# Gathering and adding the first twelve expert picks between the last query-weight tiles of a one-core Trainium2 kernel

## Chip, cores and metric

The kernel runs on one core of a Trainium2 chip. The metric is the device time of one execution in microseconds. The engines are called PE (matrix), DVE (vector), ACT (scalar), POOL (GpSimd) and SP (which only issues transfers). Each runs its own program in order and meets the others at semaphores. A difference under 0.2% of the time, some 7 us, can't be told from no change.

## The reference

Two transformer-like blocks run over 512 tokens of width 1024. The change lies in the expert layer of the first one, between the mixing output and the final norm of that block:

```python
def chunk(t):                                   # 128 tokens
    qh = (t @ w_q).reshape(T, 8, 2, 128)        # 1024 -> 2048 query features
    s = einsum('thpd,hpnd->thpn', qh, sub_keys) # 128 keys for each of 8 heads x 2 halves
    s_top, i_top = top_k(s, 16)
    cand = s_top[:, :, 0, :, None] + s_top[:, :, 1, None, :]
    best, pos = top_k(cand.reshape(T, 8, 256), 16)
    idx = ...                                   # 8 x 16 = 128 experts for each token
    g = softmax(best)
    ue, ve = u_tab[idx], v_tab[idx]             # 16384 experts x 1024, twice
    act = gelu(einsum('thkd,td->thk', ue, t))
    return einsum('thk,thkd->td', g * act, ve)
```

## The kernel before, in words

**The ring of weights.** All linear layers draw weight tiles of 1024x128 from one stream. SP loads tile n into slot n % 4 of `w32` as soon as POOL has split tile n-4. POOL splits each tile into a high and a low part (`split_tile`, L391 to L401, two instructions), once PE has finished tile n-4 (`tile_done`). PE multiplies a tile with `linear` (L474): 24 products of 128x128 by 128x512, which wait for the split of their own tile (`w_split`) and read the activations `xhi` and `xlo`.

**The query section, "pq".** It has 16 tiles m = 0 to 15. PE does the first four as one group. From then on it runs `linear` of tile m, then `key_scores(m - 1)` (L676), and for m = 4 to 7 also the turning of the tokens into rows. ACT copies each product (L1029), then the scores of the tile before (L1125). DVE finds the best keys of the first 128 tokens (`top_keys`, `top_pairs`, `pick_experts`, L1645 to L1698) as soon as four tiles of scores are there, which gives the indices of picks 0 to 31.

**The picks.** There are 512 picks: 4 groups of 128 tokens by 128 experts. For pick p POOL issues one indirect transfer (`gather`, L428), in which each of 128 partitions fetches its expert's row of `u` and of `v`, 8 KB together (1,048,576 bytes a pick). DVE makes the dot of `u` with the token (`expert_dot`, L1719). ACT makes gelu (L1158), the weight (L1162) and a diagonal matrix (L1167) of it (`expert_weight`). PE multiplies the diagonal with `v` into two banks that sum over 128 picks (`expert_sum`, L712, four recorded products a pick) and signals `pick_used`. There are eight slots for the fetched rows. They overlay split activations: `slots[0]` to `slots[3]` lie on `yhi` and `ylo`, which nobody reads any more once the section "mix" is running; `slots[4]` to `slots[7]` lie on `xhi` and `xlo`, which the query products read until tile 15 is done. A gather into a used slot waits for the `pick_used` of the pick before it there.

**The order at the seam.** POOL splits all query tiles up to number 15, then issues gathers 0 to 3, then waits at gather 4 until PE has done all 16 query tiles. ACT makes the softmax of the first 32 picks (`gates_exp(0)`, L1151) only after its last query copy; DVE waits for it before its first dot. PE does pick 0 after `key_scores(15)`. Four more weight tiles are split within the gather loop at picks 16, 24, 32 and 40, sixteen more from pick 298 on. After the last pick follow the norm and the second block. They need the sum of all picks.

Of the kernel before, what the change touches and what calls it, by code (L numbers as in the profile page):

```python
# [6 lines left out]
ALU = mybir.AluOpType  # L7
# [6 lines left out]
P = 128  # L14
# [18 lines left out]
NPICKS = T // P * PICKS  # L33
UNITS = NPICKS // UNIT
MEM_AT, MEM_EVERY = 288, 8
FF = 4096
WINDOWS = (2, 4, 8, 16)
MIX_ORDER = (1, 0, 3, 2, 5, 4, 7, 6)
# [71 lines left out]


SECTIONS, DONE, NTILES = plan()


SEMAPHORES = (
# [20 lines left out]
def build(nc, a, out):  # L136
    ctx = ExitStack()
    with ctx:
# [5 lines left out]
        def sem(name):  # L144
            return sems[name]
# [77 lines left out]
        look = flat_acc[:, 1536:2048]  # L223
        tokens = work[:, :, :].rearrange("p k t -> p (k t)").rearrange("p (t d) -> p t d", t=TT)
        dot_out = ar(12288, 1024)
        diag = flat_acc[:, 512:768].rearrange("p (a n) -> p a n", a=2)

        def peer_tokens(t):
            return tiles_of(8192 if t < 2 else 4096, 2, T)
# [36 lines left out]
        def bank(b):  # L266
            return psum[:, b, :]
# [118 lines left out]
        @block.gpsimd  # L386
        def _(pool):
            pool.memset(zeros[:, :], 0.0).then_inc(sem("zeros_set"), 1)
            pool.wait_ge(sem("zeros_set"), 1)

            def split_tile(s, n, nth, reused):  # L391

                pool.wait_ge(w_loaded[s], nth * 16)
                if reused:
                    pool.wait_ge(tile_done, n + 1 - RING)
                hi = whi[:, s, :, :].rearrange("p k n -> p (k n)")
                lo = wlo[:, s, :, :].rearrange("p k n -> p (k n)")
                pool.tensor_tensor(hi, w32[:, s, :], zeros[:, :].broadcast_to((P, 1024)), ALU.add)\  # L398
                    .then_inc(sem("w_upper"), 1)
                pool.wait_ge(sem("w_upper"), n + 1)  # L400
                pool.tensor_tensor(lo, w32[:, s, :], hi.bitcast(F32), ALU.subtract).then_inc(w_split, 1)  # L401

            for s in range(RING):
                split_tile(s, s, 1, False)

            def split_tiles(first, end):

                up, down = -(-first // RING), end // RING
                for n in range(first, up * RING):
                    split_tile(n % RING, n, n // RING + 1, True)  # L410
                with pool.Fori(up, down) as g:
                    for s in range(RING):
                        split_tile(s, g * RING + s, g + 1, True)
                for n in range(down * RING, end):
                    split_tile(n % RING, n, n // RING + 1, True)

            mixed = first_tile("pool") + RING
            n = first_tile("memk")
            split_tiles(RING, n)

            def gather(p):
                if p % UNIT == 0:
                    pool.wait_ge(sem("picked"), p // UNIT + 1)
                if p >= SLOTS:
                    pool.wait_ge(sem("pick_used"), p - SLOTS + 1)
                elif p == 4:
                    pool.wait_ge(tile_done, n)
                pool.indirect_dma_start(  # L428
                    out=slots[p % SLOTS], out_offset=None, in_=a["experts"],
                    in_offset=bass.IndirectOffsetOnAxis(ap=indices[:, p:p + 1], axis=0),  # L430
                ).then_inc(sem(f"experts_in{p % SLOTS}"), 16)

            for p in range(NPICKS):
                gather(p)
                if 16 <= p < 48 and p % 8 == 0:
                    m = (p - 16) // 8
                    split_tile((n + m) % RING, n + m, (n + m) // RING + 1, True)
                m = (p - MEM_AT - 10) // MEM_EVERY
                if p >= MEM_AT + 10 and (p - MEM_AT - 10) % MEM_EVERY == 0 and m < 2 * KB:
                    split_tile((n + RING + m) % RING, n + RING + m, (n + RING + m) // RING + 1, True)  # L440
            split_tiles(n + RING + 2 * KB, mixed)

            step = Steps(pool, "pool_step")
            pool.wait_ge(sem("affine_done"), 8 * 6 + 1)
            step(pool.memset(ppad_odd[:, :, 0:16], 0.0))
            step.settle()
            for i in range(0, 6, 2):
                k = MIX_ORDER[i]
                pool.wait_ge(sem("affine_done"), 8 * 6 + i + 1)
                mix_window(pool, step, k, ppad_odd, pool_y_odd, False)  # L450
                step(pool.tensor_tensor(yhi[:, k, :], pool_y_odd, zeros[:, :].broadcast_to((P, T)), ALU.add))
                step.settle()
                pool.tensor_tensor(ylo[:, k, :], pool_y_odd, yhi[:, k, :].bitcast(F32), ALU.subtract)\  # L453
                    .then_inc(sem("odd_split"), 1)
                pool.wait_ge(sem("odd_split"), i // 2 + 1)
            split_tiles(mixed, NTILES)
# [3 lines left out]
        def _(pe):  # L460
# [219 lines left out]
            def turn_tokens(t):  # L680
# [3 lines left out]
                for half in range(2):  # L684
# [6 lines left out]
                        mm = pe.matmul(dst, xlo[:, 4 * half + k, t * P:(t + 1) * P], identr, start=False, stop=True)  # L691
                    mm.then_inc(sem("tokens_turned"), 1)

            linear_group(n, range(o, o + 4), (sem("split2"), 0))
            for m in range(3):
                key_scores(m)
            for m in range(4, HP):
                linear(n + m, o + m)
                key_scores(m - 1)
                if m < 8:  # L700
                    turn_tokens(m - 4)
            key_scores(HP - 1)

            def expert_sum(p):

                t, c = p // PICKS, p % PICKS
                if c == 0:
                    pe.wait_ge(sem("peer_copied"), 2 * t) if t else pe.wait_ge(sem("tokens_copied"), 2 * TT)
                pe.wait_ge(sem("diagonal"), p + 1)
                v = slots[p % SLOTS][:, D:2 * D]  # L710
                for half in range(2):
                    mm = pe.matmul(bank(4 + half), diag[:, p % 2, :], v[:, half * T:(half + 1) * T], start=(c == 0),  # L712
                                   stop=(c == PICKS - 1))
                mm.then_inc(sem("pick_used"), 1)

            def turn_peer(t):

# [31 lines left out]

            MH, ML = (lambda k: mem_hi[:, k, :]), (lambda k: mem_lo[:, k, :])  # L750
            n, o = SECTIONS["memk"]
            for p in range(NPICKS):
                expert_sum(p)
                if p % PICKS == PICKS - 1:
                    turn_peer(p // PICKS)
                m, at = (p - MEM_AT) // MEM_EVERY, (p - MEM_AT) % MEM_EVERY
                if 0 <= m < 2 * KB and at == 0:
                    linear(n + m, o + m, MH, ML, CT, ready=(sem("mem_split"), 0) if m == 0 else None)
                if KB <= m < 2 * KB and at == 4:
                    pe.wait_ge(sem("peer_added"), 8 * (p // PICKS))  # L760
                    turn_copied(m - KB, SECTIONS["memv"][1], mem_raw, CT // P, 2)
# [217 lines left out]
        def _(act):  # L979
# [47 lines left out]
            def copy_product(dst, o, cols=T, func=ACT.Copy, **more):  # L1027
                wait_product(act, o)
                free(act.activation(dst, bank(o % RING)[:, 0:cols], func, **more), o)  # L1029
# [102 lines left out]
                    act.activation(tokens[:, t, half * T:(half + 1) * T], bank(4 + half), ACT.Copy)\  # L1132
                        .then_inc(sem("tokens_copied"), 1)

            act.wait_ge(sem("split2"), 8)
            for m in range(HP):
                if m >= 2:
                    act.wait_ge(sem("key_scores"), m - 1)
                copy_product(acc[:, m % 2, :], o + m)
                if m:  # L1140
                    scores_copy(m - 1)
                if 5 <= m < 9:
                    tokens_copy(m - 5)
            scores_copy(HP - 1)
            act.wait_ge(sem("key_scores"), HP)
            act.dma_start(memT, a["memT"].rearrange("(k p) t -> p k t", p=P)).then_inc(sem("mem_in"), 16)

            def gates_exp(u):
                act.wait_ge(sem("best_ready"), u + 1)
                for h in range(2):  # L1150
# [4 lines left out]
            def expert_weight(p):  # L1155
# [8 lines left out]
                act.wait_ge(sem("weighed"), p + 1)  # L1164
                if p >= 2:
                    act.wait_ge(sem("pick_used"), p - 1)
                act.activation(diag[:, p % 2, :], ident, ACT.Copy, scale=weights[:, c:c + 1])\  # L1167
                    .then_inc(sem("diagonal"), 1)

            def peer_copy(t):  # L1170
                act.wait_ge(sem("pick_used"), PICKS * (t + 1))
# [10 lines left out]
                    .then_inc(sem("values_copied"), 1)  # L1182

            n, o = SECTIONS["memk"]
            gates_exp(0)
            for p in range(NPICKS):
                expert_weight(p)
                if p % PICKS == PICKS - 1:
                    peer_copy(p // PICKS)
# [172 lines left out]
        def _(dve):  # L1362
# [346 lines left out]

            def expert_dot(p):  # L1710
                c = p % (2 * UNIT)
                dve.wait_ge(sem(f"experts_in{p % SLOTS}"), 16 * (p // SLOTS + 1))
                if p == 0:
                    dve.wait_ge(sem("tokens_copied"), 2 * TT)
                else:
                    dve.wait_ge(sem("dotted"), p)
                if p >= 2 * UNIT:
                    dve.wait_ge(sem("gelu_ready"), p - 2 * UNIT + 1)
                dve.scalar_tensor_tensor(dot_out, slots[p % SLOTS][:, 0:D], 1.0, tokens[:, p // PICKS, :], ALU.mult,  # L1719
                                         ALU.mult, accum_out=inner[:, c:c + 1]).then_inc(sem("dotted"), 1)  # L1720

            def add_peer(t):
# [422 lines left out]
```

## Time and profile before

| what | value |
|---|---|
| median of 3 runs | 3493.74 us (3491.2 to 3499.36) |
| the profiled execution, its time | 3496.58 us |
| its span | 3494.8 us |
| granted clock of PE, mean over the span | 0.928 |
| PE / DVE / POOL / ACT busy | 84% / 65% / 53% / 26% |
| ACT copies the products of query tiles 12 and 15 | at 642.36 and 661.84 us |
| pick phase, first gather after tile 15 to last gather | 662.0 to 1980.5 us |

The span is counted from the first instruction of the profile to the last; the time of the same execution is 1.8 us more. The profiled execution lies 2.8 us above the median of the runs. All stages named here by times are in us from the span's start. The granted clock is 1.0 for 2.4 GHz and 0.5 for 1.2 GHz; a busy product is not a product at its peak, since products overlap in the record.

### The profile page before, as it was taken

Reading aid. Unit: us, or ns where it says so; the run is one execution under the profiler, and the core shown is the slowest. Engines: PE = TensorE matmul, PEld = TensorE weight load, DVE = VectorE, ACT = ScalarE, POOL = GpSimd, SP = SyncE. Lnnn points to the kernel's source line nnn. Section 1 sums busy time; section 2 is a strip of 40 time slices with the busy share of each in tenths; the row PEclk is TensorE's granted clock in tenths of the full one; section 3 lists DMA queues with packets and bytes.
Section 4 is the critical chain, followed back from the end, with each engine's and each line's share of the span. In section 5 each row is a group of like instructions: output and inputs, shape, how many; then the busy total and the mean of one; then the engine's idle time right before and its main releaser. Section 6 shows DMA issues by size and latency. Waiting matters only on the chain. (4 is left out here: it accounts for less than half of the span.)

```text
span 3494.8 us, 33128 instructions
## 1 busy us (share of the span) xinstructions
PE 2945.1 (84%) x10628; PEld 1938.5 (55%) x10628; DVE 2257.4 (65%) x3761; ACT 926.1 (26%) x2350; POOL 1856.1 (53%) x1099
## 2 busy tenths in 40 slices
PE   6889898877778877888877779979899975889998
PEld 5667676632333323444433267657678864667886
DVE  7793464376666667776766583675855577586556
ACT  2115402233433333333333322221200012220001
POOL 2544375464444444666554264254577763557874
PEclk9899899999999999999999989989999987999998
DMA  5531122699999999999999811011122220112221
GB/s 216 185 113 55 43 79 73 241 421 419 413 418 412 412 422 409 391 389 399 390 422 418 341 66 55 31 60 61 60 90 96 91 72 12 61 60 93 94 96 55
DMA packets 126107, 719.21 MB, mean 206 GB/s; under 512 B 13200, under 2 KB 16400, under 8 KB 60176
## 3 DMA queue, kind: packets, MB, share of 16 engines
q0 software_dynamic: 73728, 536.90, 37.4%
q1 hardware_dynamic: 46560, 161.18, 13.4%
q10 hardware_dynamic: 5680, 19.40, 1.5%
q8 instruction: 72, 1.18, 0.1%
q14 instruction: 67, 0.55, 0.0%
HBM read 715.33 MB, written 2.10 MB: 205 GB/s over the span
## 5 line engine op out<-in xcount | busy, mean ns | idle before, releaser
L712 PE MATMUL psum<-slots,acc 128*128 128x512 f32 x2048 | 1016.2, 643 | 267.9 <-ACT acc L1167 267.4
L398 POOL TENSOR_TENSOR whi<-w,zeros 128x1024 fp32r<-128x1024 f32 x277 | 548.1, 1979 | 883.1 <-PE psum L469 566.4
L428 POOL DMA_INDIRECT slots<-in_experts,consts x512 | 564.1, 1102 | 675.0 <-PE psum L712 603.5
L1719 DVE SCALAR_TENSOR_TENSOR arena<-slots,work 128x1024 f32<-128x1024 f32 x512 | 663.2, 1295 | 400.1 <-DMA slots<-in_experts,consts 383.1
L712 PEld LDWEIGHTS psum<-slots,acc 128*128 128x128 f32 x2048 | 393.7, 202 | 868.5 <-ACT acc L1167 462.3
L401 POOL TENSOR_TENSOR wlo<-w,whi 128x1024 fp32r<-128x1024 f32 x277 | 718.2, 2593 | 21.7
L467 PE MATMUL psum<-xhi,whi 128*128 128x512 f32 x1104 | 451.5, 409 | 8.7 <-POOL wlo L401 5.6
L468 PE MATMUL psum<-xlo,whi 128*128 128x512 f32 x1104 | 441.8, 400 | 0.0
L469 PE MATMUL psum<-xhi,wlo 128*128 128x512 f32 x1104 | 440.5, 399 | 0.0
L467 PE MATMUL psum<-yhi,whi 128*128 128x512 f32 (+1 forms) x736 | 300.1, 408 | 49.9 <-POOL ylo L453 20.7
L468 PE MATMUL psum<-ylo,whi 128*128 128x512 f32 (+1 forms) x736 | 296.2, 402 | 0.0
L469 PE MATMUL psum<-yhi,wlo 128*128 128x512 f32 (+1 forms) x736 | 296.1, 402 | 0.0
L1158 ACT ACTIVATE consts<-consts 128x1 f32<-128x1 f32 x512 | 101.7, 199 | 585.2 <-DVE arena L1719 578.2
L1167 ACT ACTIVATE acc<-consts 128x128 f32<-128x128 f32 x512 | 205.5, 401 | 185.8 <-PE psum L712 172.0
L467 PEld LDWEIGHTS psum<-xhi,whi 128*128 128x128 f32 x1104 | 211.0, 191 | 66.5 <-issue 16.0
L469 PEld LDWEIGHTS psum<-xhi,wlo 128*128 128x128 f32 x1104 | 210.5, 191 | 52.0
L468 PEld LDWEIGHTS psum<-xlo,whi 128*128 128x128 f32 x1104 | 210.9, 191 | 50.5 <-issue 1.7
L1347 ACT ACTIVATE work<-psum,vecs 128x512 f32<-128x512 f32 x64 | 44.1, 689 | 579.9 <-PE psum L469 419.3
L467 PEld LDWEIGHTS psum<-yhi,whi 128*128 128x128 f32 x736 | 142.4, 193 | 92.3 <-issue 32.1
L1984 DVE TENSOR_TENSOR work<-work 128x512 f32<-128x512 f32 x64 | 108.5, 1695 | 113.8 <-ACT work L1347 113.8
L1998 DVE TENSOR_TENSOR acc<-acc,psum 128x512 f32<-128x512 f32 x112 | 75.4, 685 | 161.1 <-PE psum L469 160.9
L469 PEld LDWEIGHTS psum<-yhi,wlo 128*128 128x128 f32 x736 | 143.1, 194 | 34.6
(266 smaller groups left out, 3671.3 us busy)
## 6 DMA issues: line engine op xcount, KB each, us to landing
w<-in_stream SPq DMA_DIRECT2D x277, 512.0 KB
arena<-in_wmod SPq DMA_DIRECT2D x4, 2048.0 KB, 17.8
arena<-in_wmod ACTq DMA_DIRECT2D x8, 1024.0 KB, 6.1
acc<-in_wmod ACTq DMA_DIRECT2D x8, 1024.0 KB, 8.3
slots<-in_experts,consts POOLq DMA_INDIRECT x512
xres<-in_xT SPq DMA_DIRECT2D x1, 2048.0 KB, 15.3
outT<-xres SPq DMA_DIRECT2D x8, 256.0 KB, 2.0
consts<-in_consts SPq DMA_DIRECT2D x1, 1056.0 KB, 5.2
```

Source lines behind the costliest of these rows:

```text
L398: pool.tensor_tensor(hi, w32[:, s, :], zeros[:, :].broadcast_to((P, 1024)), ALU.add)\
L401: pool.tensor_tensor(lo, w32[:, s, :], hi.bitcast(F32), ALU.subtract).then_inc(w_split, 1)
L428: pool.indirect_dma_start(out=slots[p % SLOTS], out_offset=None, in_=a["experts"], in_offset=bass.IndirectOffsetOnAxis(ap=indices[:, p:p + ...
L467: pe.matmul(dst, hi, xh(k), start=(j == 0), stop=False)
L468: pe.matmul(dst, hi, xl(k), start=False, stop=False)
L469: mm = pe.matmul(dst, lo, xh(k), start=False, stop=(j == len(ks) - 1))
L712: mm = pe.matmul(bank(4 + half), diag[:, p % 2, :], v[:, half * T:(half + 1) * T], start=(c == 0), stop=(c == PICKS - 1))
L1158: act.activation(gelus[:, c:c + 1], inner[:, c:c + 1], ACT.Gelu).then_inc(sem("gelu_ready"), 1)
L1167: act.activation(diag[:, p % 2, :], ident, ACT.Copy, scale=weights[:, c:c + 1])\
L1719: dve.scalar_tensor_tensor(dot_out, slots[p % SLOTS][:, 0:D], 1.0, tokens[:, p // PICKS, :], ALU.mult, ALU.mult, accum_out=inner[:, c:c + ...
L1984: step(dve.tensor_tensor(q, t, t, ALU.mult))
L1998: free(dve.tensor_tensor(acc[:, k, :], acc[:, k, :], bank(oo % RING), ALU.add), oo)
```

## The change

The first twelve picks use only `slots[0]` to `slots[3]`, three times each; from pick 12 on the slots go round as before. POOL splits the query tiles only up to number 11 ahead. Then it issues gathers 0 to 3, splits tile 12, issues gathers 4 and 5, splits tile 13, issues 6 and 7, splits tile 14, issues 8 and 9, splits tile 15, issues 10 and 11, and goes on from pick 12. Gather 4 waits until pick 0 has been added, gather 5 for pick 1, and so on. PE adds picks 0 and 1 after the product of tile 12 and `key_scores(11)`, picks 2 and 3 after tile 13, 4 and 5 after tile 14, 6 and 7 after tile 15, and the rest as before. ACT makes the softmax of the first 32 picks at tile 9, and the weights of two picks after each of tiles 12 to 15. The diagonals of the first twelve picks have a place of their own, since the old one is the buffer of the query copies. DVE's order stays as it is.

```diff
--- before.py
+++ after.py
@@ -33,6 +33,7 @@
 NPICKS = T // P * PICKS
 UNITS = NPICKS // UNIT
 MEM_AT, MEM_EVERY = 288, 8
+FIRST, FIRST_AT = 12, 12
 FF = 4096
 WINDOWS = (2, 4, 8, 16)
 MIX_ORDER = (1, 0, 3, 2, 5, 4, 7, 6)
@@ -112,6 +113,20 @@
 SECTIONS, DONE, NTILES = plan()
 
 
+def slot_uses():
+
+    slots = [p % 4 if p < FIRST else (p - FIRST + 4) % SLOTS for p in range(NPICKS)]
+    before, uses, last = [], [], {}
+    for p, slot in enumerate(slots):
+        before.append(last.get(slot))
+        uses.append(slots[:p + 1].count(slot))
+        last[slot] = p
+    return slots, before, uses
+
+
+SLOT, SLOT_BEFORE, SLOT_USES = slot_uses()
+
+
 SEMAPHORES = (
     "tile_done", "early_done", "bank_free0", "bank_free1", "bank_free2", "bank_free3", "w_loaded0", "w_loaded1",
     "w_loaded2", "w_loaded3", "w_split", "consts_in", "vecs_in", "ctx_in", "conds_in", "mod_dot", "mod_in0",
@@ -223,7 +238,10 @@
         look = flat_acc[:, 1536:2048]
         tokens = work[:, :, :].rearrange("p k t -> p (k t)").rearrange("p (t d) -> p t d", t=TT)
         dot_out = ar(12288, 1024)
-        diag = flat_acc[:, 512:768].rearrange("p (a n) -> p a n", a=2)
+        diags = [t.rearrange("p (a n) -> p a n", a=2) for t in (ar(9216, 256), flat_acc[:, 512:768])]
+
+        def diag(p):
+            return diags[p >= FIRST][:, p % 2, :]
 
         def peer_tokens(t):
             return tiles_of(8192 if t < 2 else 4096, 2, T)
@@ -416,21 +434,28 @@
 
             mixed = first_tile("pool") + RING
             n = first_tile("memk")
-            split_tiles(RING, n)
 
             def gather(p):
                 if p % UNIT == 0:
                     pool.wait_ge(sem("picked"), p // UNIT + 1)
-                if p >= SLOTS:
-                    pool.wait_ge(sem("pick_used"), p - SLOTS + 1)
-                elif p == 4:
-                    pool.wait_ge(tile_done, n)
+                if SLOT_BEFORE[p] is not None:
+                    pool.wait_ge(sem("pick_used"), SLOT_BEFORE[p] + 1)
+                else:
+                    pool.wait_ge(tile_done, n if p >= FIRST else first_tile("mix"))
                 pool.indirect_dma_start(
-                    out=slots[p % SLOTS], out_offset=None, in_=a["experts"],
+                    out=slots[SLOT[p]], out_offset=None, in_=a["experts"],
                     in_offset=bass.IndirectOffsetOnAxis(ap=indices[:, p:p + 1], axis=0),
-                ).then_inc(sem(f"experts_in{p % SLOTS}"), 16)
-
-            for p in range(NPICKS):
+                ).then_inc(sem(f"experts_in{SLOT[p]}"), 16)
+
+            early = first_tile("pq") + FIRST_AT
+            split_tiles(RING, early)
+            for p in range(4):
+                gather(p)
+            for m in range(4):
+                split_tile((early + m) % RING, early + m, (early + m) // RING + 1, True)
+                for p in range(4 + 2 * m, 6 + 2 * m):
+                    gather(p)
+            for p in range(FIRST, NPICKS):
                 gather(p)
                 if 16 <= p < 48 and p % 8 == 0:
                     m = (p - 16) // 8
@@ -691,6 +716,18 @@
                         mm = pe.matmul(dst, xlo[:, 4 * half + k, t * P:(t + 1) * P], identr, start=False, stop=True)
                     mm.then_inc(sem("tokens_turned"), 1)
 
+            def expert_sum(p):
+
+                t, c = p // PICKS, p % PICKS
+                if c == 0:
+                    pe.wait_ge(sem("peer_copied"), 2 * t) if t else pe.wait_ge(sem("tokens_copied"), 2 * TT)
+                pe.wait_ge(sem("diagonal"), p + 1)
+                v = slots[SLOT[p]][:, D:2 * D]
+                for half in range(2):
+                    mm = pe.matmul(bank(4 + half), diag(p), v[:, half * T:(half + 1) * T], start=(c == 0),
+                                   stop=(c == PICKS - 1))
+                mm.then_inc(sem("pick_used"), 1)
+
             linear_group(n, range(o, o + 4), (sem("split2"), 0))
             for m in range(3):
                 key_scores(m)
@@ -699,19 +736,10 @@
                 key_scores(m - 1)
                 if m < 8:
                     turn_tokens(m - 4)
+                if m >= FIRST_AT:
+                    expert_sum(2 * (m - FIRST_AT))
+                    expert_sum(2 * (m - FIRST_AT) + 1)
             key_scores(HP - 1)
-
...
 
             def turn_peer(t):
 
@@ -749,7 +777,7 @@
 
             MH, ML = (lambda k: mem_hi[:, k, :]), (lambda k: mem_lo[:, k, :])
             n, o = SECTIONS["memk"]
-            for p in range(NPICKS):
+            for p in range(2 * (HP - FIRST_AT), NPICKS):
                 expert_sum(p)
                 if p % PICKS == PICKS - 1:
                     turn_peer(p // PICKS)
@@ -1132,19 +1160,6 @@
                     act.activation(tokens[:, t, half * T:(half + 1) * T], bank(4 + half), ACT.Copy)\
                         .then_inc(sem("tokens_copied"), 1)
 
...
-
             def gates_exp(u):
                 act.wait_ge(sem("best_ready"), u + 1)
                 for h in range(2):
@@ -1164,8 +1179,26 @@
                 act.wait_ge(sem("weighed"), p + 1)
                 if p >= 2:
                     act.wait_ge(sem("pick_used"), p - 1)
-                act.activation(diag[:, p % 2, :], ident, ACT.Copy, scale=weights[:, c:c + 1])\
+                act.activation(diag(p), ident, ACT.Copy, scale=weights[:, c:c + 1])\
                     .then_inc(sem("diagonal"), 1)
+
+            act.wait_ge(sem("split2"), 8)
+            for m in range(HP):
+                if m >= 2:
+                    act.wait_ge(sem("key_scores"), m - 1)
+                copy_product(acc[:, m % 2, :], o + m)
+                if m:
+                    scores_copy(m - 1)
+                if 5 <= m < 9:
+                    tokens_copy(m - 5)
+                if m == 9:
+                    gates_exp(0)
+                if m >= FIRST_AT:
+                    expert_weight(2 * (m - FIRST_AT))
+                    expert_weight(2 * (m - FIRST_AT) + 1)
+            scores_copy(HP - 1)
+            act.wait_ge(sem("key_scores"), HP)
+            act.dma_start(memT, a["memT"].rearrange("(k p) t -> p k t", p=P)).then_inc(sem("mem_in"), 16)
 
             def peer_copy(t):
                 act.wait_ge(sem("pick_used"), PICKS * (t + 1))
@@ -1182,8 +1215,7 @@
                     .then_inc(sem("values_copied"), 1)
 
             n, o = SECTIONS["memk"]
-            gates_exp(0)
-            for p in range(NPICKS):
+            for p in range(2 * (HP - FIRST_AT), NPICKS):
                 expert_weight(p)
                 if p % PICKS == PICKS - 1:
                     peer_copy(p // PICKS)
@@ -1709,14 +1741,14 @@
 
             def expert_dot(p):
                 c = p % (2 * UNIT)
-                dve.wait_ge(sem(f"experts_in{p % SLOTS}"), 16 * (p // SLOTS + 1))
+                dve.wait_ge(sem(f"experts_in{SLOT[p]}"), 16 * SLOT_USES[p])
                 if p == 0:
                     dve.wait_ge(sem("tokens_copied"), 2 * TT)
                 else:
                     dve.wait_ge(sem("dotted"), p)
                 if p >= 2 * UNIT:
                     dve.wait_ge(sem("gelu_ready"), p - 2 * UNIT + 1)
-                dve.scalar_tensor_tensor(dot_out, slots[p % SLOTS][:, 0:D], 1.0, tokens[:, p // PICKS, :], ALU.mult,
+                dve.scalar_tensor_tensor(dot_out, slots[SLOT[p]][:, 0:D], 1.0, tokens[:, p // PICKS, :], ALU.mult,
                                          ALU.mult, accum_out=inner[:, c:c + 1]).then_inc(sem("dotted"), 1)
 
             def add_peer(t):
```

## Rows read from the trace of the kernel before

**Rows 1.** The page: DMA busy tenths, the span in 40 equal slices.

```profile
DMA  5531122699999999999999811011122220112221
```

**Rows 2.** Stretches: length, busy of each engine, granted clock, DMA share, GB/s.

```profile
611.00:616.00 5.00, 5.00 (x23) 4.04 (x22) 0.00 (x0) 0.00 (x0) 0.00 (x0) 1.00 0.32 105
655.00:662.00 7.00, 7.00 (x38) 5.86 (x37) 0.00 (x0) 1.36 (x3) 0.00 (x0) 1.00 0.01 5
...
663.00:1983.00 1320.00, 1052.30 (x2453) 443.69 (x2453) 910.91 (x2029) 503.33 (x1646) 659.29 (x547) 0.93 1.00 410
1950.00:1980.00 30.00, 23.95 (x49) 8.13 (x48) 14.79 (x24) 10.95 (x37) 11.26 (x12) 1.00 1.01 421
```

**Rows 3.** Waits, 600 to 2000 us: total, times, longest.

```profile
DVE small L1702 <- ACT consts L1151: 63.9, 1, 63.9
```

**Rows 4.** POOL's timeline: start, length, [idle before, releaser].

```profile
608.62 2.37 POOL L401 TENSOR_TENSOR wlo<-w,whi 128x1024 fp32r<-128x1024 f32 x1
616.37 1.89 POOL L398 TENSOR_TENSOR whi<-w,zeros 128x1024 fp32r<-128x1024 f32 x1 [5.38 <-PE psum L469]
...
622.93 1.89 POOL L398 TENSOR_TENSOR whi<-w,zeros 128x1024 fp32r<-128x1024 f32 x1 [2.18 <-PE psum L469]
624.90 2.40 POOL L401 TENSOR_TENSOR wlo<-w,whi 128x1024 fp32r<-128x1024 f32 x1
```

**Rows 5.** POOL's timeline at the seam and after it.

```profile
640.46 1.17 POOL L428 DMA_INDIRECT slots<-in_experts,consts  x1 [0.17 <-issue]
...
644.42 0.93 POOL L428 DMA_INDIRECT slots<-in_experts,consts  x1 [0.30 <-issue]
662.01 0.94 POOL L428 DMA_INDIRECT slots<-in_experts,consts  x1 [16.66 <-PE psum L469]
...
687.91 1.16 POOL L428 DMA_INDIRECT slots<-in_experts,consts  x1 [0.77 <-PE psum L712]
689.63 0.94 POOL L428 DMA_INDIRECT slots<-in_experts,consts  x1 [0.56 <-PE psum L712]
```

**Rows 6.** DVE's timeline: the first indices, and what follows them.

```profile
603.13 0.18 DVE L1698 CAST consts<-consts 128x32 uint32<-128x32 f32 x1
667.21 0.17 DVE L1702 RECIPROCAL small<-small 128x2 f32<-128x2 f32 x1 [63.90 <-ACT consts L1151]
```

**Rows 7.** ACT's timeline: copies of tile 12 and 13, and the first weight.

```profile
642.36 0.60 ACT L1029 ACTIVATE acc<-psum 128x512 f32<-128x512 f32 x1 [5.06 <-PE psum L469]
643.19 0.60 ACT L1125 ACTIVATE arena<-psum 128x512 f32<-128x512 f32 x1 [0.23 <-PE psum L676]
648.85 0.60 ACT L1029 ACTIVATE acc<-psum 128x512 f32<-128x512 f32 x1 [5.06 <-PE psum L469]
...
667.19 1.28 ACT L1158 ACT_TABLE_LOAD   x1
668.90 0.20 ACT L1158 ACTIVATE consts<-consts 128x1 f32<-128x1 f32 x1 [0.42 <-DVE arena L1719]
```

**Rows 8.** PE's timeline: after key scores 15, and after a short pause.

```profile
670.07 11.24 PE L712 MATMUL psum<-slots,acc 128*128 128x512 f32 x20 [5.53 <-ACT acc L1167]
...
697.12 11.38 PE L712 MATMUL psum<-slots,acc 128*128 128x512 f32 x20 [4.57 <-ACT acc L1167]
```

**Rows 9.** Stretches again, columns as in rows 2: products at either clock.

```profile
544.00:548.00 4.00, 4.00 (x10) 3.12 (x10) 3.90 (x9) 2.15 (x3) 0.00 (x0) 0.50 0.00 0
550.00:554.00 4.00, 4.00 (x19) 3.22 (x18) 3.90 (x9) 1.64 (x2) 0.00 (x0) 1.00 0.18 25
...
668.00:675.00 7.00, 4.93 (x6) 2.18 (x7) 6.58 (x14) 3.56 (x12) 0.67 (x1) 0.51 1.02 416
675.00:680.00 5.00, 5.00 (x13) 2.23 (x12) 4.79 (x31) 1.19 (x4) 2.14 (x3) 1.00 1.03 374
```

**Rows 10.** POOL's timeline: the last two gathers.

```profile
1977.99 0.94 POOL L428 DMA_INDIRECT slots<-in_experts,consts  x1 [1.54 <-PE psum L712]
1980.47 0.94 POOL L428 DMA_INDIRECT slots<-in_experts,consts  x1 [1.55 <-PE psum L712]
```

More of the change, by code:

```diff
@@ L701, in _ @@
                     turn_tokens(m - 4)
+                if m >= FIRST_AT:
+                    expert_sum(2 * (m - FIRST_AT))
+                    expert_sum(2 * (m - FIRST_AT) + 1)
             key_scores(HP - 1)
[L704 to L714, printed above, removed]
             def turn_peer(t):
@@ L1133, in tokens_copy @@
                         .then_inc(sem("tokens_copied"), 1)
[L1135 to L1146, printed above, removed]
             def gates_exp(u):
```

## The prediction

> **What bounds the kernel now.** I read the page's slices first, since one busy share can't speak for a program of so many stages. The DMA digits stand at 9 for fourteen slices, from the ninth to the 22nd, and at 2 or less nearly everywhere after that [rows 1]. That block is the pick phase. The table by stretches then says how full it is: over the 1320 us from 663 to 1983 the DMA engines are busy with share 1.00 at 410 GB/s, and with share 1.01 at 421 GB/s near the end, while no engine is full [rows 2]. A gather is 1,048,576 bytes, so at 421 GB/s it should take 2.49 us; the last two are issued 2.48 us apart [rows 10]. So from the first gather after tile 15 (662.01) to the last (1980.47) the chip moves bytes and the rest follows. What sets the time of this phase is when it starts and how many gathers are left by then.
>
> Before it, the query section is bound by PE: ACT's copies of tiles 12 and 13 come 6.49 us apart, each after 5.06 us of idleness that PE ends [rows 7]. POOL's splits have slack here: it waits 5.38 and 2.18 us for PE before it may split [rows 4]. The DMA is idle at the end of it (share 0.01 from 655 to 662) [rows 2], because four gathers were issued by 645.35 and the fifth, at 662.01, waits for tile 15 [rows 5]. The indices for all of them had been there since 603.31; DVE then sat 63.90 us until ACT came to the softmax [rows 3, 6]. So there is room: some 50 us in which twelve gathers (30 us of transfer) would fit. The question is what the new order makes of PE's section.
>
> **The change part by part.** *Gathers 0 to 3 earlier.* POOL is done with tile 11 at 608.62 + 2.37 = 610.99 and idle until 616.37, when tile 8 is done [rows 4]. Four issues took 640.46 to 645.35, 4.89 us [rows 5]. They fit into that gap of 5.38 us, so split 12 stays at 616.37 and costs nothing; the DMA has share 0.32 there [rows 2]. They are four gathers that before too had landed before 655, so they save nothing by themselves.
>
> *Softmax at tile 9.* Two small exponentials and a table load, in ACT's idle of about 5 us a tile [rows 7]. Zero; if it were not hidden, 2 us. DVE's dots 0 to 3 then run long before PE wants them; gather 4 will be issued at 648 and its dot is wanted at about 684, so DVE, which has its next top-k work behind that dot, is covered too. The gelu table load of 1.28 us [rows 7] moves between the score copy and the first weight, where PE waits for it: once 1.28 us.
>
> *The new waits on POOL.* This is the part that decides. Gather 4 waits for pick 0, gather 5 for pick 1, and both come after PE's product of tile 12. Behind them in POOL's order stands the split of tile 13, which before ran at 622.93, twenty microseconds ahead of PE [rows 4, 7]. PE's next product waits for that split. So after each pair of picks PE, POOL and ACT run one after the other. From ACT's copy of one tile to the copy of the next:
>
> - copy to end of the score copy: 643.19 + 0.60 - 642.36 = 1.43 us [rows 7]
> - gelu, weight, diagonal, first product of PE: 670.07 - 668.90 = 1.17 us [rows 7, 8]
> - two picks on PE: twice 689.63 - 687.91 = 1.72, so 3.44 us (gathers that wait for slots follow PE's picks at that distance) [rows 5]
> - issue of the odd gather: 0.95 us [rows 5]
> - split: 624.90 + 2.40 - 622.93 = 4.37 us [rows 4], and 0.1 us to PE (my estimate)
> - the 24 products to the copy: 6.49 less the 0.83 between copy and score copy = 5.66 us [rows 7]
>
> That is 17.1 us in place of 6.49.
>
> *The clock.* In each round PE is idle for 0.95 + 4.37 + 0.1 = 5.4 us before its products. When PE had been idle for 5.53 us, the granted clock was 0.51 over 668 to 675, though PE worked again from 670.07, and 1.00 in the stretch after [rows 8, 9]. The same products come 10 in 4 us at clock 0.50 and 19 in 4 us at 1.00 [rows 9]. PE so loses half of some 4.9 us, 2.4 us a round. With it a round is 19.5 us. (The Trainium skill, "TensorE: Matmul & The Clock Gate", section "Seeing it yourself", warns that clock records have been unreliable. If they were so here, the term would vanish and the sum be that of the first rival below; the count of products agrees with the records.)
>
> *The sum up to the saturated phase.* Copy 12 stays at 642.36. Copy 13 comes after 19.5 + 1.28 at 663.1, copy 14 at 682.6, copy 15 at 702.1 (before 661.84). Pick 6 is added 1.43 + 1.17 + 1.72 later, at 706.5, and there gather 10 is issued. Gather 11 follows 1.7 us later, and 12 to 15 at once behind it, since tile 15 is done. Gathers 16 and 17 need picks 8 and 9, which landed long ago and are added by about 715; six gathers are 15 us of transfer, so the DMA doesn't run dry. Had this cover gone, each gather that came late would cost its 2.5 us. From gather 10 on the phase is as full as it was from gather 4 at 662.01.
>
> *What is given back.* Six gathers (4 to 9) are already done by then: 6 x 2.48 = 14.9 us [rows 10]. (By the Trainium skill, "DMA: Bandwidth & Descriptors", section "Anatomy of one DMA", bytes move at 436 GB/s: 2.40 us a gather, an estimate by which 14.4 us would come back and the sum be half a microsecond more.) The bounds of this term: 0, if they save nothing, and 6 x 1320/508 = 15.6 us, the average over the 508 gathers, which holds other transfers as well [rows 2, 5].
>
> Start of the phase 706.5 - 662.0 = +44.5, less 14.9: **+29.6 us**. Everything behind the phase shifts with it unchanged. Of the +44.5, 31.9 us are three rounds that grew by 10.6, 7.2 us the clock, 1.3 us the table, and the rest is that the saturated phase now starts behind the sum of pick 6 and not at tile 15 itself. Against the profiled execution, 3496.58 + 29.6 = 3526.2 us; that execution lies 2.8 us above the median of the runs, so **3523.3 us**, which I round to 3523.
>
> **The rivals.**
>
> - *No clock fall.* Before the pauses seen, PE had other work behind it than it will have now, so it might keep its clock over 5.4 us. Then +22.4 us, 3516. Against it: a pause of 4.57 us within the picks was followed by five picks in 11.38 us, as slow as the first five (11.24), where the pace of 1.72 gives 8.6 [rows 8].
> - *A deeper fall.* PE also idles 3.1 us between key scores 11 and pick 0, and the clock may not recover before the next pause. The bound is a tile wholly at half clock, 5.66 instead of 2.4 lost, thrice 3.3, and 2.7 us for slow first picks [rows 8]: +42 us at most, 3536; halfway 3530.
> - *The early gathers save nothing.* If the phase's length hung on something other than bytes, the delay would come through whole: +44.5, 3538. Against it stands share 1.00 over 1320 us [rows 2].
> - *Not slower: a fuller stream.* The mean rate of the phase is 410 GB/s and its best 421 [rows 2]. If the picks done ahead left DVE, ACT and PE so far in front that no burst of top-k work or split ever thins the stream again, the phase would take 1320 x 410/421, 34.5 us less: -5 us, 3489. It decides from 419.5 GB/s on, where the gain is 29.6. Against it: from pick 12 on the slots and their waits are the same as before, so the lead over the DMA is again eight slots at most, and the share is already 1.00.
>
> That the change doesn't do what it says is not open: POOL's waits stand in program order ahead of the splits.
>
> **How the numbers follow.** Chances: forecast 0.68, no clock fall 0.14, deeper fall 0.10, nothing saved 0.05, fuller stream 0.03. The range starts at 3512, below the no-fall case by 4 us for a split, an issue or a latency that is shorter than its row, and ends at 3533, between the forecast and the deep end of the second rival; outside are half of that rival and the last two, some 0.14. One per cent is 35 us, and 0.2% is 7 us, which is about what can be told from no change: only the fuller stream, and a delay that I overlooked a cover for, lie there. Slower 0.95, same 0.03, faster 0.02.
>
> **What the profile after would show.** Right: gathers 0 to 3 at 611 to 616; the splits of tiles 13, 14 and 15 at about 650.6, 670 and 689, each right behind a gather, with PE's products waiting for them (a wait of PE on the low split, three times, about 5 us each); PE's clock near 0.5 in the first 5 us of each of these tiles; gather 10 at about 706 and the last gather at about 2010; GB/s in the phase still 410. Wrong: splits that run ahead of the picks; a phase whose rate differs by more than 1%; or products at full clock after the pauses.

## Result and profile after

The changed kernel takes 3524.79 us (median of 6 runs, 3517.37 to 3530.16) against 3492.47 us for the kernel before (6 runs): a ratio of 1.0092, 95% interval 1.0076 to 1.0108, or +32.3 us where +29.6 was worked out. Timed a second time, beside other runs of the kernel before, it took 3527.41 us against 3490.84 us, ratio 1.01 (1.0084 to 1.0115), or +36.6 us. The profiled execution has a span of 3522.9 us. Its slices answer to [rows 1]; the block of nines begins as before in the ninth slice of a longer span:

```profile
DMA  5531122299999999999999911111122220112221
```

Single executions differ in what they need up to the seam: the copy of tile 12 lies at 642.36 us before the change and at 636.67 in this trace, and between 636 and 644 in those of the experiments that add no more than two picks before it. So I count from that copy.

POOL's timeline after, which answers to [rows 4] and [rows 5] (start, length, idle time before and what ended it):

```profile
605.54 1.17 POOL L445 DMA_INDIRECT slots<-in_experts,consts  x1 [0.17 <-issue]
...
610.75 1.89 POOL L416 TENSOR_TENSOR whi<-w,zeros 128x1024 fp32r<-128x1024 f32 x1 [0.32 <-PE psum L494]
612.72 2.41 POOL L419 TENSOR_TENSOR wlo<-w,whi 128x1024 fp32r<-128x1024 f32 x1
643.32 0.96 POOL L445 DMA_INDIRECT slots<-in_experts,consts  x1 [28.20 <-PE psum L727]
646.22 0.94 POOL L445 DMA_INDIRECT slots<-in_experts,consts  x1 [1.94 <-PE psum L727]
647.18 1.90 POOL L416 TENSOR_TENSOR whi<-w,zeros 128x1024 fp32r<-128x1024 f32 x1
649.15 3.22 POOL L419 TENSOR_TENSOR wlo<-w,whi 128x1024 fp32r<-128x1024 f32 x1
664.38 0.96 POOL L445 DMA_INDIRECT slots<-in_experts,consts  x1 [12.01 <-PE psum L727]
...
684.21 0.96 POOL L445 DMA_INDIRECT slots<-in_experts,consts  x1 [12.55 <-PE psum L727]
...
704.17 0.96 POOL L445 DMA_INDIRECT slots<-in_experts,consts  x1 [12.98 <-PE psum L727]
...
2004.94 0.94 POOL L445 DMA_INDIRECT slots<-in_experts,consts  x1 [1.54 <-PE psum L727]
```

Gathers 0 to 3 lie between the splits of tiles 11 and 12, where POOL stood idle before. Then POOL stands for 28.20 us at gather 4, with the split of tile 13 behind it. It stands for 12.01 us at gather 6 and for 12.55 us at gather 8, with the splits of tiles 14 and 15 behind them. The split of tile 13 starts 0.02 us after the issue of gather 5. Of the first twelve picks ten are gathered before gather 10, the first of the full phase, and six are added before tile 15 is done. ACT's copies of tiles 12 to 15 answer to [rows 7]:

```profile
636.67 0.60 ACT L1057 ACTIVATE acc<-psum 128x512 f32<-128x512 f32 x1 [5.06 <-PE psum L494]
659.78 0.60 ACT L1057 ACTIVATE acc<-psum 128x512 f32<-128x512 f32 x1 [18.50 <-PE psum L494]
679.62 0.60 ACT L1057 ACTIVATE acc<-psum 128x512 f32<-128x512 f32 x1 [16.70 <-PE psum L494]
699.58 0.60 ACT L1057 ACTIVATE acc<-psum 128x512 f32<-128x512 f32 x1 [16.83 <-PE psum L494]
```

Rounds of 23.11, 19.84 and 19.96 us stand where 6.49 was. PE's timeline shows the two pauses of a round, one before the picks and one before the next tile's products:

```profile
640.58 5.37 PE L727 MATMUL psum<-slots,arena 128*128 128x512 f32 x8 [3.11 <-ACT arena L1182]
652.42 0.80 PE L492 MATMUL psum<-xhi,whi 128*128 128x512 f32 x1 [6.48 <-POOL wlo L419]
...
662.12 3.70 PE L727 MATMUL psum<-slots,arena 128*128 128x512 f32 x8 [1.54 <-ACT arena L1182]
```

The waits of 600 to 712 us (total, times, longest) show how the second pause adds up, and DVE's wait for the softmax, which answers to [rows 3]:

```profile
DVE small L1734 <- ACT consts L1166: 23.0, 1, 23.0
...
PE psum L492 <- POOL wlo L419: 18.0, 3, 6.5
```

And the stretches (length, busy of PE, PEld, DVE, ACT, POOL with counts, granted clock, DMA share, GB/s), which answer to [rows 2] and [rows 9]:

```profile
643.00:646.00 3.00, 2.94 (x5) 0.86 (x3) 0.00 (x0) 0.00 (x0) 0.96 (x1) 0.62 0.36 66
...
672.00:676.00 4.00, 4.00 (x10) 3.13 (x11) 1.98 (x4) 0.00 (x0) 0.00 (x0) 0.50 0.40 135
676.00:680.00 4.00, 4.00 (x21) 3.32 (x21) 0.00 (x0) 0.38 (x1) 0.00 (x0) 1.00 0.02 4
...
710.00:2026.00 1316.00, 1041.91 (x2445) 437.87 (x2443) 904.14 (x1988) 497.31 (x1628) 648.82 (x538) 0.94 0.99 408
```

The products of tile 14 come 10 in 4 us at half clock, then 21 in 4 us; the first pair of picks is slowed too (0.62). The phase is as full as before: 408 against 410 GB/s.

The bill: from the copy of tile 12, gather 10 comes after 67.50 us, where gather 4 came after 19.65. That is +47.9. From there to the last gather it takes 1300.8 us in place of 1318.5, -17.7. In all +30.2 us. The rest of the two traces differs too: the copy of tile 12 comes 5.7 us earlier after the change, and behind the last gather the program takes 1518.0 us in place of 1514.3. These three terms add up to the 28.1 us between the spans. The last of them can't be charged to the change: over all traces of this case that rest takes 1514.3 to 1520.6 us, and the trace before is the shortest of them.

### The profile page after: what moved, and what is told of

Read it like the earlier page. It is cut to its first block and busy times, and to the rows that moved or that the text cites. A ratio compares the mean times of both kernels' runs of the same rounds, so it can differ in the third digit from the quotient of the medians.

```text
span 3522.9 us, 33122 instructions
## 1 busy us (share of the span) xinstructions
PE 2947.2 (84%) x10628; PEld 1941.8 (55%) x10628; DVE 2261.2 (64%) x3761; ACT 925.8 (26%) x2350; POOL 1855.0 (53%) x1099
## 5 line engine op out<-in xcount | busy, mean ns | idle before, releaser
L727 PE MATMUL psum<-slots,acc 128*128 128x512 f32 x2000 | 984.5, 639 | 264.3 <-ACT acc L1182 261.9
L1751 DVE SCALAR_TENSOR_TENSOR arena<-slots,work 128x1024 f32<-128x1024 f32 x512 | 673.2, 1315 | 464.7 <-DMA slots<-in_experts,consts 449.3
L727 PEld LDWEIGHTS psum<-slots,acc 128*128 128x128 f32 x2000 | 380.6, 200 | 847.3 <-ACT acc L1182 460.2
L493 PEld LDWEIGHTS psum<-ylo,whi 128*128 128x128 f32 x736 | 143.3, 195 | 33.9 <-issue 0.2
## 6 DMA issues: line engine op xcount, KB each, us to landing
arena<-in_wmod SPq DMA_DIRECT2D x4, 2048.0 KB, 17.7
```

The costliest lines, as they stand in the source:

```text
L493: pe.matmul(dst, hi, xl(k), start=False, stop=False)
L727: mm = pe.matmul(bank(4 + half), diag(p), v[:, half * T:(half + 1) * T], start=(c == 0), stop=(c == PICKS - 1))
L1751: dve.scalar_tensor_tensor(dot_out, slots[SLOT[p]][:, 0:D], 1.0, tokens[:, p // PICKS, :], ALU.mult, ALU.mult, accum_out=inner[:, c:c + 1] ...
```

## Experiments

Each was timed in several rounds beside runs of the kernel before on the same chip. Ratios are to that kernel, with 95% intervals.

**Splits ahead of the waiting gathers.** One edit to the changed kernel:

```diff
             for m in range(4):
                 split_tile((early + m) % RING, early + m, (early + m) // RING + 1, True)
-                for p in range(4 + 2 * m, 6 + 2 * m):
-                    gather(p)
+            for p in range(4, FIRST):
+                gather(p)
```

> The changed kernel with one edit: POOL splits the query tiles 12 to 15 before it waits at gather 4, and issues gathers 4 to 11 after them. Theory (the splits queued behind the waiting gathers make the rounds long): a round from ACT's copy of one tile to the next falls from 19.5 to 11.8 us (1.43 score copy, 1.17 to PE, 3.44 for two picks, 5.66 for the products), no clock fall before the products, gather 10 about 21 us later than the kernel before issued gather 4 (measured from the copy of tile 12), less 14.9 given back: +6 to +9 us against the kernel before, 25 us less than the changed kernel, near 3500 us. Rival (the rounds are long because of the picks themselves, on ACT and PE): within 3 us of the changed kernel, near 3525 us.

Measured: 3501.72 us against 3495.08, ratio 1.0017 (1.0008 to 1.0026), +6.6 us. ACT's copies in its trace:

```profile
642.59 0.60 ACT L1057 ACTIVATE acc<-psum 128x512 f32<-128x512 f32 x1 [5.06 <-PE psum L494]
...
657.56 0.60 ACT L1057 ACTIVATE acc<-psum 128x512 f32<-128x512 f32 x1 [10.35 <-PE psum L494]
...
669.29 0.60 ACT L1057 ACTIVATE acc<-psum 128x512 f32<-128x512 f32 x1 [8.60 <-PE psum L494]
...
681.01 0.60 ACT L1057 ACTIVATE acc<-psum 128x512 f32<-128x512 f32 x1 [8.59 <-PE psum L494]
```

The rounds are 14.97, 11.73 and 11.72 us long, with 11.8 expected. The first is 3.2 us longer than the others, which I hadn't allowed for: PE waits 3.11 us for the first diagonal in place of 1.54, and the first two picks take it 5.37 us in place of 3.70. Counted from the copy of tile 12, tile 15 is copied 24.5 us sooner than in the changed kernel, and the time against the kernel before falls from +32.3 to +6.6, within the +6 to +9 that I gave. The order of splits and gathers on POOL, with the clock falls that follow from it, makes some 25 us.

**Idle products in the pauses.** Behind each of the first three pairs:

```diff
                     expert_sum(2 * (m - FIRST_AT) + 1)
+                    if m + 1 < HP:
+                        for j in range(20):
+                            pe.matmul(bank(7), identr, xhi[:, j % KB, :], start=True, stop=True)
```

> The changed kernel with twenty products of no use (the identity by slices of xhi, into bank 7, which nobody reads then) behind each of the first three pairs of picks, 4.7 us at full clock, so that PE isn't idle while POOL splits. It adds work and changes no result. Theory (PE loses some 2 us a round to the lower clock after each pause): granted clock 1.0 in the products of tiles 13 to 15, 5 to 7 us less than the changed kernel, near 3519 us. Rival (the clock costs nothing that counts, or the fillers are in the way): the same as the changed kernel or up to 5 us more.

Measured: 3523.64 us against 3495.08, ratio 1.008 (1.0067 to 1.0094), where I had expected some 3519 us. The interval overlaps that of the changed kernel, so the time decides nothing. The trace says more. The same stretch of tile 14 as above, in this kernel:

```profile
672.00:676.00 4.00, 4.00 (x19) 3.22 (x18) 1.23 (x2) 0.00 (x0) 0.00 (x0) 1.00 0.28 110
```

The clock is full, and the rounds are 20.89, 17.90 and 17.65 us long, 6.5 less in all. So both kernels were timed again, beside each other:

> The changed kernel itself, so that the next run and it share a chip and the runs of the kernel before. +29 to +33 us against the kernel before, near 3524 us.

> The kernel with the idle products once more, beside the changed kernel. In the trace of its first run the rounds were 6.5 us shorter in all. Theory (the lower clock costs time on the path): 4 to 8 us less than the changed kernel in the same job. Rival (the shortened rounds are given back): within 2 us of it.

Measured: changed kernel 3527.41 us, ratio 1.01 (1.0084 to 1.0115), +36.6 us, above the +29 to +33 that I gave; with idle products 3519.26 us, ratio 1.0082 (1.0069 to 1.0095). The medians are 8.2 us apart and the rounds of the two traces 7.0 us (64.36 against 57.40 from the copy of tile 12 to that of 15). Both times the traces with idle products show the clock at 1.0 in the products of tiles 13 to 15, and rounds that are shorter by nearly the same amount. From the copy of tile 12 to the last gather these traces are 8.8 and 9.1 us shorter than those of the changed kernel. So useless work in the pauses shortens this stage, since PE then meets its real work at full clock. That the whole time falls with it is likely and no more, for the intervals of the ratios just overlap.

**No gather ahead.** One edit to the kernel before:

```diff
-                elif p == 4:
+                elif p == 0:
                     pool.wait_ge(tile_done, n)
```

> The kernel before with one edit: gathers 0 to 3 too wait until PE is done with query tile 15, so no pick is fetched ahead. Theory (the phase is bound by bytes and a gather done ahead of it is worth 2.48 us): four gathers more in the phase, +9.9 us against the kernel before, near 3502 us. Rival (what is fetched ahead saves nothing, the phase hangs on something else): 0 to +3 us.

Measured: 3504.16 us against 3495.08, ratio 1.0025 (1.0016 to 1.0034), +9.1 us by the medians. Four gathers moved into the full phase cost 2.3 us each. The credit for gathers done ahead is real.

**The front alone.** The changed kernel with `FIRST` = 4, all splits ahead, and sums and weights behind tile 15 as before:

```diff
-FIRST, FIRST_AT = 12, 12
+FIRST, FIRST_AT = 4, 12
...
-                if m >= FIRST_AT:
-                    expert_sum(2 * (m - FIRST_AT))
-                    expert_sum(2 * (m - FIRST_AT) + 1)
```

> The changed kernel with only its front: gathers 0 to 3 are issued ahead of split 12 and the softmax stands at tile 9, all splits run ahead, no pick is added and no fifth gather issued before tile 15 is done. Theory (these parts lie in idle time and save nothing, since the four gathers were through in time before too): -2 to +2 us against the kernel before, near 3494 us. Rival (the earlier dots of DVE and the softmax off the seam shorten the start of the phase): -5 us or more.

Measured: 3496.27 us against 3490.84, ratio 1.0009 (0.9999 to 1.0018). The medians are 5.4 us apart, outside the +-2 us I gave, but the interval holds 1. In its trace the way from the copy of tile 12 to the last gather is 3.0 us shorter than before (1335.1 for 1338.1), so time and trace point opposite ways. No gain from the earlier gathers and softmax can be seen in the time, and no loss that can be told from none.

**Weights a tile ahead, five pairs.** The splits as in the first experiment, sums at tiles 11 to 15 (`FIRST_AT` = 11), and on ACT:

```diff
-                if m >= FIRST_AT:
-                    expert_weight(2 * (m - FIRST_AT))
-                    expert_weight(2 * (m - FIRST_AT) + 1)
+                if FIRST_AT - 1 <= m < HP - 1:
+                    expert_weight(2 * (m + 1 - FIRST_AT))
+                    expert_weight(2 * (m + 1 - FIRST_AT) + 1)
```

> The changed kernel with the splits of tiles 12 to 15 ahead, and with ACT making the weights of a pair one tile before PE adds it: ACT at tiles 11 to 14 after the score copy, PE at tiles 11 to 15, five pairs in place of four. PE then should wait for nobody. Theory: tile 15 is done 4 x 3.44 = 13.8 us later than in the kernel before, gathers 4 to 11 (8 x 2.48 = 19.8 us) are through by then: -6 us against the kernel before, near 3486 us. Rival (a pick before tile 15 costs PE as much as it saves the DMA, since the phase has slack): 0 to +5 us.

> The kernel with five pairs and ready weights once more, beside the former on one chip and one set of runs of the kernel before: -6 to -10 us.

The edit puts ACT's weights at tiles 10 to 14; the first expectation names 11 to 14 for five pairs, which is a slip.

Measured: 3485.35 us against 3495.08, ratio 0.9975 (0.9963 to 0.9986), and again 3487.81 against 3494.16, ratio 0.9979 (0.9971 to 0.9988). It beats the kernel before by 6 to 10 us. In its first trace the tiles from 11 to 15 follow each other every 9.9 us on average, as 6.49 + 3.44 says, and PE's clock stays at 1.0 from 600 to 680 us. A part of that:

```profile
660.00:672.00 12.00, 12.00 (x54) 8.61 (x53) 4.79 (x10) 3.92 (x10) 2.90 (x3) 1.00 0.62 231
```

**Seven pairs.** The same with sums at tiles 9 to 15, sixteen picks in the four slots:

> As the kernel with ready weights, with seven pairs in place of five: softmax at tile 7, weights at tiles 8 to 14, sums at tiles 9 to 15, the first sixteen picks in the four free slots, splits always ahead of the gather that would block them. DVE's first dot waits for the first two token copies alone, its others follow it. Theory: tile 15 is done 6 x 3.44 = 20.6 us later than in the kernel before, twelve more gathers (29.8 us) are through: -9 us against the kernel before, near 3485 us, and some 3 us less than with five pairs. Rival (more picks ahead collide with the token turning or with DVE's first top-k work): no better than five pairs, or worse.

Measured: 3482.55 us against 3490.84, ratio 0.9975 (0.9967 to 0.9984): -8.3 us, where five pairs gave -9.7 and -6.4. Its trace showed a hole in the issues just when the last slots came free:

```profile
682.52 1.29 POOL L445 DMA_INDIRECT slots<-in_experts,consts  x1 [4.38 <-PE psum L498]
683.83 1.90 POOL L416 TENSOR_TENSOR whi<-w,zeros 128x1024 fp32r<-128x1024 f32 x1
685.81 3.22 POOL L419 TENSOR_TENSOR wlo<-w,whi 128x1024 fp32r<-128x1024 f32 x1
689.18 0.96 POOL L445 DMA_INDIRECT slots<-in_experts,consts  x1
```

> The kernel with seven pairs, and the four weight tiles that POOL splits among the gathers moved from picks 16, 24, 32, 40 to 24, 32, 40, 48. In the trace with seven pairs POOL issued one gather after tile 15 (682.5) and then split for some 5 us before the next (689.2), while the DMA ran dry. Theory (that hole ate what two more pairs brought): 3 to 6 us less than seven pairs, -11 to -14 us against the kernel before. Rival (the hole is made good within the phase): -8 us, as with five or seven pairs.

That the DMA ran dry in the hole was too strongly put: its share was 0.72, 0.79 and 0.74 in the three stretches of 3 us from 682 to 691.

Measured: 3486.2 us against 3494.16, ratio 0.9975 (0.9963 to 0.9986), -8.0 us. The hole is gone from the trace and the time hasn't moved, so my theory of the hole isn't borne out. It isn't refuted either, because this trace shows a loss of another kind, as large as the gain I had hoped for. After dot 4 DVE does its next top-k work, and the weight of pick 5 waits for the dot behind it. It is the collision that the rival of the seven pairs named:

```profile
642.07 0.20 ACT L1177 ACTIVATE consts<-consts 128x1 f32<-128x1 f32 x1 [8.95 <-DVE arena L1755]
```

PE then waited 3.99 us for that diagonal, and the copies of tiles 10 and 11 lie 16.3 us apart in place of 9.9. In the trace with seven pairs before it they were 10.7 us apart, so this loss doesn't come every time.

The traces can be compared from the copy of tile 8, which all of them pass before the first pick, to the last gather. That takes 1364.1 us in the kernel before, 1351.2 and 1353.0 with five pairs, 1349.7 with seven, and 1356.9 with seven and late splits. So seven pairs were 1.5 to 3.4 us shorter in the one trace without that loss. Whether they gain more than five isn't settled: each of the four intervals is 6 to 8 us wide, and 3 us are in question.

## Why the prediction was right, and where it was off

The sign, the mechanism and the size were right: the rounds that the forecast describes are the ones that the traces show. By its steps:

- *Gathers 0 to 3 and softmax for nothing.* They fit the gap, and the front alone shows no gain. DVE's wait for the softmax fell from 63.90 to 23.0 us, to no avail.
- *The blocked splits.* Shown by the order in the trace and by the first experiment, which takes away that order and with it some 25 us.
- *The size of a round.* Second and third: 19.84 and 19.96 for 19.5. First: 23.1 for 20.8. The forecast put a slow start of the picks at nothing, and here the second rival was right in one place. After 3.11 us of idleness PE did the first two picks in 5.37 us, at a clock of 0.62 from 643 to 646. Gather 5, which waits for the second of them, was issued 5.64 us after PE began, where I had 3.44: +2.2 us. The low split took 3.22 us, not 2.40, and the split with the way to PE 5.24 us, not 4.47: +0.8. Against that the clock was back 3.3 us into tile 13, sooner than the 4.9 us I had charged: -0.7.
- *The clock.* 7.2 us charged for three tiles; 6.5 and 7.0 us in the rounds of two pairs of traces. In the changed kernel's own trace the products of tiles 13, 14 and 15 take 7.36, 7.90 and 8.33 us up to the copy, where 5.66 is the time at full clock: 6.6 us in all. The rival without a fall is out by the traces' clock, and the rival of a deeper one holds for the first pair of picks only.
- *Start of the phase.* +47.9 for +44.5. Of the 3.4 us in excess, 3.1 lie in the three rounds (62.91 for 59.8).
- *Given back.* 17.7 for 14.9. The phase needs 2.60 us a gather in either trace, as it holds other transfers too, by which six gathers are 15.6 us. From gather 10 to the last the changed kernel's two traces and the three of its variants with the same order behind gather 10 take 1298.4 to 1302.7 us, so a miss of 2.8 us can't be told from none. The rival that nothing is saved is out by the experiment without gathers ahead. The rival of a fuller stream is out by 408 GB/s.

The two misses nearly cancel, +3.4 and -2.8, and that is luck: it brings the trace to +30.2, within 1 us of the forecast. The rest of the measured +32.3 against +29.6 is within the interval, which is 11 us wide, and the second timing gave +36.6. One small sum in the chances is off: the cases outside the range are 0.05 + 0.05 + 0.03, 0.13 and not 0.14.

What the change lacked is seen in the five pairs: the same idea pays once the splits run ahead and the weights are made a tile before PE wants them. (No run tells the ready weights from the fifth pair.) A pick then costs PE 1.72 us ahead of the phase and takes 2.3 to 2.5 us of transfer out of it.

## What to carry to other kernels

Before an operation with a new wait is put into an engine's order, look at what stands behind it there and who needs that: here a gather that waited for PE held back the weight split that PE needed next, and a hidden 4.4 us became part of a 20 us round. Work moved ahead of this phase, which is bound by transfers, was worth its bytes and no more (2.3 us a gather), and the delay of the phase's start came through in full. Issue what is ready first, and what waits last.

## What the hardware showed beside

PE's clock fell after an idleness of only 3.11 us here, and it fell late. It was still 1.00 when PE began the picks, from 640.5 to 641.5 us, and stood at 0.50 from 642 to 645. In the later rounds the pause before the picks was 1.54 us and the clock stayed at 1.00 (662 to 666). Idle products that nobody reads held it at 1.0 for the tiles' products and took 6.5 and 7.0 us off the rounds.

POOL's low split and DVE's dot seem to stretch each other. Alone the split takes some 2.4 us and the dot 1.23. Beside the split of tile 13 DVE's dot began first, at 648.80, 0.35 us before the low split: the dot took 1.37 us and the split 3.22. At tile 14 the split began first, and it was the dot that grew (lines of both engines' timelines, the last dot with no split beside it):

```profile
648.80 1.37 DVE L1751 SCALAR_TENSOR_TENSOR arena<-slots,work 128x1024 f32<-128x1024 f32 x1 [22.47 <-DMA slots<-in_experts,consts]
...
669.32 2.34 POOL L419 TENSOR_TENSOR wlo<-w,whi 128x1024 fp32r<-128x1024 f32 x1
669.91 2.83 DVE L1751 SCALAR_TENSOR_TENSOR arena<-slots,work 128x1024 f32<-128x1024 f32 x1 [13.01 <-DMA slots<-in_experts,consts]
...
673.11 1.22 DVE L1751 SCALAR_TENSOR_TENSOR arena<-slots,work 128x1024 f32<-128x1024 f32 x1 [0.35 <-DMA slots<-in_experts,consts]
```

The four traces of the changed kernel and of the one with idle products hold twelve such overlaps, one for each of the tiles 13 to 15. In two of them the dot began first: it took 1.37 and 1.23 us, and the split 3.22 and 3.34. In ten the split began first: it took 2.34 to 2.39 us, and the dot 2.11 to 3.32. That the one slows the other is what these times suggest, and no run took either away.
